# Differential attention in a two-block kernel on one core: all four score rows of heads 1 to 3 in one group, dense gate tiles in one bank

## The reference

```python
def one(inp):
    qb, start = inp
    allowed = _chunk_visible(start, Q_BLOCK, T)
    logits = jnp.einsum('bqhcd,bshcd->bhcqs', qb, k, preferred_element_type=F32) * DIFF_HD ** -0.5
    logits = jnp.where(allowed, logits, -jnp.inf)
    p = jax.nn.softmax(logits, axis=-1)
    attn = (p[:, :, 0] - lam * p[:, :, 1]).astype(v.dtype)
    return jnp.einsum('bhqs,bshd->bqhd', attn, v)
...
log_a = jax.nn.log_sigmoid((a_lr @ wa2 + ba).astype(F32)) / GLA_TAU
```

## Time and profile before

| | |
|---|---|
| median of 3 runs | 1878.92 us |
| profiled execution, its own time | 1878.7 us |
| its span | 1876.9 us |
| TensorE busy | 1872.6 us (100%) |
| weight loads busy | 1546.0 us (82%) |
| VectorE busy | 1180.9 us (63%) |
| ScalarE busy | 890.0 us (47%) |
| GpSimd busy | 336.2 us (18%) |

### The profile page before, as it was taken

The page is one execution under the profiler, slowest core; times in us unless marked ns, Lnnn a source line. Parts: engine busy times, 40 slices in busy tenths (PEclk is TensorE's granted clock), DMA queues, the critical chain, the costliest instruction groups (busy, mean ns, idle before and its releaser), DMA issues.

```text
span 1876.9 us, 25233 instructions
## 1 busy us (share of the span) xinstructions
PE 1872.6 (100%) x9681; PEld 1546.0 (82%) x9681; DVE 1180.9 (63%) x1955; ACT 890.0 (47%) x1430; POOL 336.2 (18%) x172
## 2 busy tenths in 40 slices
PE   9999999999999999999999999999999999999999
PEld 7977788788888888788888888888788888888887
DVE  7777557684553567787656736466589655755553
ACT  6564566543332445534445553445543444545442
POOL 1010012121120121343010010131235110010211
PEclk9999999999999999999999999999999999999999
DMA  6211114223222233122122123223222213122321
GB/s 241 96 68 68 46 46 157 90 90 112 90 96 106 90 134 135 68 105 97 46 100 81 68 82 124 90 98 149 90 90 90 82 54 112 46 93 90 132 93 68
DMA packets 26891, 178.94 MB, mean 95 GB/s; under 512 B 3232, under 2 KB 4128, under 8 KB 6560
## 3 DMA queue, kind: packets, MB, share of 16 engines
q1 hardware_dynamic: 24768, 163.99, 24.1%
q10 hardware_dynamic: 2016, 13.51, 1.9%
HBM read 171.19 MB, written 6.29 MB: 95 GB/s over the span
## 4 chain that ended last, share of the span: by engine, by line
PE 100%; DVE 0%; DVEq 0%; issue 0%
PE pp L284 34%; PE pp L288 17%; PE pp L274 10%; PE pp L275 10%; PE pp L276 10%; PE po L284 4%; PE po L288 2%; PE po L937 1%; PE po L1222 1%; PE pt L903 1%; PE ps L817 1%; PE ps L1294 1%; PE po L1162 1%; PE pt L1186 0%; PE pt L1207 0%; PE ps L1242 0%
## 5 line engine op out<-in xcount | busy, mean ns | idle before, releaser
L268 DVE TENSOR_TENSOR wlo<-wraw,whi 128x2048 fp32r<-128x2048 f32 x123 | 286.2, 2327 | 221.9 <-ACT whi L263 221.2
L263 ACT ACTIVATE whi<-wraw 128x2048 fp32r<-128x2048 f32 x150 | 286.5, 1910 | 47.2 <-PE pp L288 47.1
L284 PE MATMUL pp<-hhi,whi 128*128 128x512 f32 (+1 forms) x693 | 279.7, 404 | 0.0
L284 PE MATMUL pp<-hlo,whi 128*128 128x512 f32 (+1 forms) x693 | 270.6, 391 | 0.0
L288 PE MATMUL pp<-hhi,wlo 128*128 128x512 f32 (+1 forms) x693 | 187.2, 390 | 0.0
L284 PE MATMUL pp<-whi,hhi 128*128 128x512 f32 x464 | 187.0, 403 | 0.0
L284 PE MATMUL pp<-whi,hlo 128*128 128x512 f32 x464 | 181.2, 391 | 0.0
L2043 POOL TENSOR_TENSOR wlo<-wraw,whi 128x2048 fp32r<-128x2048 f32 x26 | 120.2, 4623 | 230.9 <-ACT whi L263 230.9
L274 PE MATMUL pp<-split,whi 128*128 128x512 f32 x402 | 156.8, 390 | 0.0
L284 PEld LDWEIGHTS pp<-hhi,whi 128*128 128x128 f32 (+1 forms) x693 | 130.0, 188 | 32.3 <-issue 6.0
L276 PE MATMUL pp<-split,wlo 128*128 128x512 f32 x402 | 156.4, 389 | 0.0
(11 more groups left out here) (472 smaller groups left out, 3447.6 us busy)
## 6 DMA issues: line engine op xcount, KB each, us to landing
wraw<-weights SPq DMA_DIRECT2D x150, 1024.0 KB, 4.8
out_t<-xT ACTq DMA_DIRECT2D x4, 1024.0 KB, 3.9
xT<-out_t ACTq DMA_DIRECT2D x2, 2048.0 KB, 8.2
wraw<-weights SPq DMA_DIRECT2D x8, 256.0 KB, 6.4
work<-cmp_w ACTq DMA_DIRECT2D x1, 2048.0 KB, 9.2
xT<-x_t ACTq DMA_DIRECT2D x1, 2048.0 KB, 7.8
xT<-x_t SPq DMA_DIRECT2D x3, 512.0 KB, 8.5
out_t<-xT SPq DMA_DIRECT2D x3, 512.0 KB, 2.6
```

The lines of the kernel that those rows point to most:

```text
L263: nc.scalar.activation(whi[:, slot, :], wraw[:, slot, :], ACT.Copy).then_inc(w_hi, 1)
L268: nc.vector.tensor_tensor(wlo[:, slot, :], wraw[:, slot, :], whi[:, slot, :].bitcast(F32), ALU.subtract).then_inc(w_lo, 1)
L284: nc.tensor.matmul(out_ap, *pair, start=(start and n == 0 and part == 0), stop=False)
```

## The change

Three things change.

1. In heads 1 to 3 row 3 of the scores joins rows 0 to 2 at `i` = 0 (`diff_rows`). Its two maps go to other banks: the second half of the `pp` pair and `po[(s - 1) % 2]` (`diff_bank`). The second of those is the bank to which the value products of head `s - 1` go, so TensorE waits for the exponentials of that row before it starts them. VectorE combines rows 0 and 1 before it takes the maxima of row 3, all of it at `i` = 0. ScalarE takes the exponentials of row 3 there too.
2. Dense gate tiles 2 to 7 all use one bank (`gate_bank`). Each tile from the fourth on (and the first `gk` tile after them) waits until the one before it is copied out. In heads 1 to 3 the first quarter of the second tile is issued after the value products and transposes of `i` = 2 instead of ahead of them.
3. The small product with `wa2` contracts over 17 rows instead of 128, and `alr_f` is filled with ones on 32 partitions instead of 128.

```diff
@@ pe_tile_part
-                pe.wait_ge(evac, t0 + n - 1)
+                pe.wait_ge(evac, t0 + n - (0 if name == "cgate" and n >= 3 else 1))
...
+            bank = gate_bank(l, n) if name == "cgate" else pp[(par0 + n) % 2]
@@ by_bank
-            return [r for r in (rows[:2], rows[2:]) if r]
+            return [r for r in (rows[:2], rows[2:3], rows[3:]) if r]
@@ diff_rows
-            return ((0, 1, 2), (), (), (3,))[u] if s == 0 else ((0, 1, 2), (), (3,), ())[u]
+            return ((0, 1, 2), (), (), (3,))[u] if s == 0 else ((0, 1, 2, 3), (), (), ())[u]
@@ diff_bank
+            if s > 0 and i == 3:
+                return pp[(par_of("cgate", l)[0] + 1) % 2] if g else po[(s - 1) % 2]
             return pt[g] if i == 2 else ps[g]
+        def gate_bank(l, m):
+            return pp[(par_of("cgate", l)[0] + (m if m < 2 else 0)) % 2]
@@ pe_tm_tile
-            pe.wait_ge(evac, t0 + n - 1)
+            pe.wait_ge(evac, t0 + n - (0 if name == "gk" and n == 0 else 1))
@@ pe_score_diff
-            elif i in (0, 3):
+            elif i == 0 or s == 0 and i == 3:
                 pe.wait_ge(ex_done, n)
+            elif i == 3 and s == 1:
+                pe.wait_ge(evac, section("cgate", l)[2] + 2)
@@ pe_layer
-                        pe_tile_part(pe, "cgate", l, 2 * s + i // 2, 2 * (i % 2), 4)
+                        if s == 0 or i != 2:
+                            pe_tile_part(pe, "cgate", l, 2 * s + i // 2, 2 * (i % 2), 4)
...
+                    if 1 <= s < 4 and i == 2:
+                        pe.wait_ge(ex_done, 4 * (U1 + 12 * l + 4) + 8 * s + 7)
...
+                    if 1 <= s < 4 and i == 2:
+                        pe_tile_part(pe, "cgate", l, 2 * s + i // 2, 0, 4)
...
-                last = nc.tensor.matmul(pt[i // 2][:, 256 * (i % 2):256 * (i % 2) + 256], alr_f[:, i * P:i * P + P],
-                                        wa2_f, start=True, stop=True)
+                last = nc.tensor.matmul(pt[i // 2][:, 256 * (i % 2):256 * (i % 2) + 256], alr_f[0:17, i * P:i * P + P],
+                                        wa2_f[0:17, :], start=True, stop=True)
@@ act_layer
-                        nc.scalar.activation(gate_c[m], pp[(par0 + m) % 2][:, :], ACT.Copy).then_inc(evac, 1)
+                        nc.scalar.activation(gate_c[m], gate_bank(l, m)[:, :], ACT.Copy).then_inc(evac, 1)
@@ dve_layer
-                        if s > 0 and i == 1:
-                            dve_combine(dve, l, s, 0)
                         for rows in by_bank(diff_rows(s, i)):
-                            dve_masked_max_pair(dve, 4 * (U1 + 12 * l + 4) + 8 * s, diff_bank, s, rows, mask_chunk)
+                            if s > 0 and rows[0] == 3:
+                                dve_combine(dve, l, s, 0)
+                                dve_combine(dve, l, s, 1)
+                            dve_masked_max_pair(dve, 4 * (U1 + 12 * l + 4) + 8 * s,
+                                                lambda s, i, g: diff_bank(l, s, i, g), s, rows, mask_chunk)
...
-                        if s > 0 and i == 1:
-                            dve_combine(dve, l, s, 1)
@@ pool
-            nc.gpsimd.memset(alr_f[:, :], 1.0)
+            nc.gpsimd.memset(alr_f[0:32, :], 1.0)
```

More of the change, by code:

```diff
@@ L383, in pe_tile_part @@
             cc = slice(m * P, m * P + P)
-            last = high_first(pe, c0 + k, pp[(par0 + n) % 2][:, :], [
+            bank = gate_bank(l, n) if name == "cgate" else pp[(par0 + n) % 2]
+            last = high_first(pe, c0 + k, bank[:, :], [
                 ((wh[:, x, cc], wl[:, x, cc]), (hhi[:, x, :], hlo[:, x, :]), lambda: None)
@@ L795, in diff_values, with diff_bank @@
                     (2,) if s == 4 else (1,))[u]
-        def diff_bank(s, i, g):
+        def diff_bank(l, s, i, g):
+            if s > 0 and i == 3:
+                return pp[(par_of("cgate", l)[0] + 1) % 2] if g else po[(s - 1) % 2]
             return pt[g] if i == 2 else ps[g]
+        def gate_bank(l, m):
+            return pp[(par_of("cgate", l)[0] + (m if m < 2 else 0)) % 2]
         def turn_at(kb):
@@ L1293, in pe_score_diff @@
                     rows = y_rows(g)
-                    last = nc.tensor.matmul(diff_bank(s, i, g)[:, at:at + w], qr[s % 2][x][rows, i * P:i * P + P],
+                    last = nc.tensor.matmul(diff_bank(l, s, i, g)[:, at:at + w], qr[s % 2][x][rows, i * P:i * P + P],
                                             kr[s % 2][y][rows, 0:w], start=(x + y == 0 and i != 1),
@@ L1306, in act_exp_diff @@
                     dst = p2_f[i] if g else attn(s)[:, STEP * i:STEP * i + w]
-                    nc.scalar.activation(dst, diff_bank(s, i, g)[:, SC_AT[i]:SC_AT[i] + w], ACT.Exp, bias=pnmx[s % 2][:, c:c + 1],
+                    nc.scalar.activation(dst, diff_bank(l, s, i, g)[:, SC_AT[i]:SC_AT[i] + w], ACT.Exp, bias=pnmx[s % 2][:, c:c + 1],
                                          accum_out=psum_[s % 2][:, c:c + 1]).then_inc(ex_done, 1)
```

## The result

The changed kernel takes **1881.99 us** (median of 20 runs, 1881.76 to 1882.46), the kernel before 1878.88 (20 runs beside them, 1878.56 to 1880.84). The ratio is 1.0016, with a 95% interval of 1.0011 to 1.0022: 3.11 us or 0.17% slower, which is within 0.2% and the side that was forecast. The forecast's 1881.4 was 0.6 too low.

The account below looks back on a forecast made before the run. TensorE, busy 1872.6 of 1876.9 us, was taken to bound the kernel. Merging -2.7, waits +4.4 and the 17-row product +0.8 summed to +2.5 us, giving 1881.4 us, 0.13% slower, verdict the same, range 1877.2 to 1883.5.

Parts of the forecast that it names:

- Row 3 inside the group still costs its 0.65: Score groups of heads 1 to 3: row 3 keeps 0.65 us but loses its 0.45 border, saving 2.7 us over six groups.
- Head 2, wait 1.14: Transposes of the next queries at `i` = 1 wait 1.14 us for VectorE's reading of head 0's output, now last.
- Head 1, wait 0.12: Value products at `i` = 2 of head 1 wait 0.12 us for ScalarE's copy of transposed weights.
- Head 3 and the end: Head 3's value products wait 0.55 us for copied weights; the first `gk` tile waits 0.37 for gate tile 7's copy.
- The 17 rows: The `wa2` product, now of another height between 128-row dense tiles, costs 0.4 us a layer, 0.8 in all.
- The quarter tile that splits the small products: Dense quarter moved behind the value products, splitting heads 1 and 2's small products: taken at nothing, bounds 0 to 1.8 us.
- the allowance: An estimated 0.15 us for signal and weight load ahead of a waiting matmul; at 0 the waits were 1.7 a layer.
- the chain is later: Rival: exponentials or combines in heads 1 to 3 each run 0.4 us later, adding 2.4, so 1883.8 us; chance 0.12.
- the clock falls after a wait: Rival: a half-speed stretch after head 2's wait in each layer costs 2 x 2.7 us, so 1886.9; chance 0.05.
- The waits fall away: Rival: the chain, above all head 2's output reading, runs earlier, so 1877.0 us; chance 0.19 for 1876.5 to 1879.8.
- The merged group keeps its price: Rival: row 3's cost comes from its new banks, not array height, so the 2.7 us don't come: 1884.1; chance 0.03.

Follow-up runs that it names:

- the experiment with waits of 2.3 to 2.7 us: The changed kernel, with VectorE reading the finished output ahead of the combines in heads 2 and 3: 1894.14 us, ratio 1.0082 to the kernel before.

## Why the prediction was right, and where it was off

The verdict, the side, and the mechanism held: the merged row saves its border, and the banks that it takes make later work wait for more than that. A table of each layer, as worked out ahead and as the trace has it (head to head from the first score row, so it holds all the small shifts):

| term, us per layer | predicted | measured |
|---|---|---|
| three merged rows | -1.35 | -1.20 |
| head 1, value products | +0.12 | +0.25 |
| head 2, queries, and what follows | +1.14 | +1.19 |
| head 3, value products; loop's end | +0.55, +0.37 | +0.93 together |
| `wa2` product and rest | +0.40 | +0.37 |
| sum | +1.23 | +1.54 |

Twice 1.54 is 3.1, the difference of the medians. The measured rows come from first scores to first scores: heads 1 and 2 took 17.89 and 17.88 before and 17.74 and 18.67 now; the entry of each is that difference with 0.40 added for the merged row. Head 3's runs from its first scores to the first `gk` matmul, 16.88 before and 17.41 now.

- *"Row 3 inside the group still costs its 0.65"*: it costs 0.70. This term of the sum was mis-sized by 0.05 a group, 0.3 us in all. The 0.65 came from counting columns; the excursion, 1.10 as a whole, was read rightly, so the border is 0.40 and not 0.45.
- *Head 2, wait 1.14*: 1.05, and 0.14 more behind it. VectorE's dates were right to 0.1, though by luck in one respect. The combines were priced from head 0, with no GpSimd beside them. In head 2 of the kernel before GpSimd did run beside them (from 1047.91, for 1.04), and L1317 took 0.99 there and not 0.22:

```profile
1047.97 0.99 DVE L1317 SCALAR_TENSOR_TENSOR nst<-nst,stat 128x1 f32<-128x1 f32 x1
```

  In the changed kernel GpSimd starts behind the output's reading, which now comes last, so the short price was the right one. The prediction saw that GpSimd's work comes later, and found that nothing waits for it; that it also sets VectorE free was missed. Undone in one experiment, it cost 12 us.
- *Head 1, wait 0.12*: the wait itself is 0.13, as dated. The products start at 1034.58 where the dense stream would let them start at 1034.00 + 0.45 = 1034.45, and although the view of waits puts their gap of 0.36 down to "issue", it ends 0.11 behind ScalarE's copy of the weights:

```profile
1033.83 0.60 ACT L1222 ACTIVATE work<-pt 128x512 f32<-128x512 f32 x1
1034.54 0.97 PEld L1229 LDWEIGHTS po<-work 128*128 128x128 f32 x8 [0.36 <-issue]
```

  The sum didn't have the rest of the 0.25: from the eight products to the next three it takes 0.96 behind such a wait and 0.89 without one, and some 0.05 are small shifts behind them.
- *Head 3 and the end*: 0.52 and 0.36 against 0.55 and 0.37; undone singly they gave 0.71 and 0.63 for two layers.
- *The 17 rows*: 0.8 predicted, 0.85 alone and 0.74 in the changed kernel. The Trainium skill, TensorEngine Tiling (Array Packing), section Key Properties, has the drain at a change of mode, and the trace agrees: a gap of 0.35 going in, and one of 0.33 coming out. Its section Performance Considerations would put 17 and 64 rows into different modes; no difference in price shows between them.
- *The quarter tile that splits the small products*: taken at nothing. No gap stands at its borders.
- *Sums that don't come out*: with the allowance at 0 the four waits sum to 1.6 a layer and not 1.7, and with every chain 0.25 later to 3.2 and not 3.1. In "the chain is later" the places are three a layer, six in all, as the working 2 x (0.4 x 3) has it, and not five. None of this moves the forecast.

The changed kernel in windows of 2 us behind head 2's wait, the granted clock again behind POOL:

```profile
1052.00:1054.00 2.00, 2.00 (x14) 1.74 (x14) 1.04 (x3) 1.30 (x3) 1.76 (x2) 1.00 0.00 0
```

Of the rivals, "the clock falls after a wait" did not happen: behind the 1.05 us of head 2 the window of the changed kernel reads 1.00. It did in the experiment with waits of 2.3 to 2.7 us. So the clock can fall in this loop, and behind the waits of the change it did not; no run has a wait between 1.1 and 2.3 us there. Its price was taken too high, 2.7 us a stretch where the experiment has 1.6. "The waits fall away" did not happen either: all four are there. "The merged group keeps its price" fell: the group of four costs 2.31, not 2.7. "The chain is later" did not decide; VectorE's came 0.08 later, not 0.22.

## What to carry to other kernels

Merging a small piece of work of another height into a group saves only its border (here 0.40 us each), and a bank taken for it turns into waits at the next users of that bank: date those users before making the change. Going to a shorter contraction among full ones cost two borders here and saved nothing: the eight products took as long over 17 rows as over 64, and 0.4 a layer longer in all than over 128. Before an order is changed on one engine, look at what its last output releases on the others: GpSimd, released 3 us earlier, turned an order that costs 0.6 us without it into one that costs 12.

## What the runs showed of the hardware

- A VectorE operation of one column, `SCALAR_TENSOR_TENSOR`, took 0.99 us beside a GpSimd `TENSOR_TENSOR` and 0.22 without; on 128 columns 1.31 against 0.35.
- A GpSimd `TENSOR_TENSOR` that started 0.05 us behind a VectorE `TENSOR_TENSOR` of 2.28 us took 3.14 us; elsewhere the same shape took 1.04.
- The granted clock fell to 0.50 for some 3 us behind three of four TensorE waits of 2.3 to 2.7 us, and behind none of the loop's waits of up to 1.1 us.
- A wait of TensorE that had long been met cost nothing; behind one met 0.1 us late, eight small products also took 0.07 us longer to the next group (0.96 against 0.89).
- A product over 17 or 64 rows between matmuls over 128 rows: the same gaps, 0.35 us ahead of its weight loads and 0.33 behind, and the same 1.59 us for its eight loads.
